# A 96-byte larger scratch tile ahead of the work area: every tile behind it moves by 96 bytes

## The reference

```
for layer in range(DEPTH):                      # DEPTH = 4
    g = norm_g[layer]
    ff = swiglu(rmsnorm(h, g[0]), ffn_w_in[layer, 0], ffn_w_out[layer, 0])
    h = h + 0.5 * rmsnorm(ff, g[1])
    u = rmsnorm(h, g[2])
    m = mixer(u)          # layers 0, 3: window attention; 1: gated linear attention; 2: rwkv
    h = h + rmsnorm(m, g[3])
    ff = swiglu(rmsnorm(h, g[4]), ffn_w_in[layer, 1], ffn_w_out[layer, 1])
    h = h + 0.5 * rmsnorm(ff, g[5])

def swiglu(x, w_in, w_out):                     # w_in 1024 x 5632, w_out 2816 x 1024
    gate, up = jnp.split(x @ w_in, 2, axis=-1)
    return (jax.nn.silu(gate) * up) @ w_out
```

## Time and profile before

| | |
|---|---|
| time, median of 3 | 3388.44 us (3382.83 to 3391.96) |
| the profiled execution's own time | 3391.96 us |
| its span | 3390.2 us |
| TensorE busy | 3270.2 us, 96% |
| VectorE, ScalarE, GpSimd busy | 1961.5, 1518.3, 175.0 us |
| chain that ended last | TensorE 85%, VectorE 8%, ScalarE 5% |
| transfers | 522.06 MB, mean 154 GB/s |

### The profile page before, as it was taken

The page is one execution under the profiler, slowest core; times in us unless marked ns, Lnnn a source line. Parts: engine busy times, 40 slices in busy tenths (PEclk is TensorE's granted clock), DMA queues, the critical chain, the costliest instruction groups (busy, mean ns, idle before and its releaser), DMA issues.

```text
span 3390.2 us, 49870 instructions
## 1 busy us (share of the span) xinstructions
PE 3270.2 (96%) x21454; PEld 2885.9 (85%) x21454; DVE 1961.5 (58%) x2964; ACT 1518.3 (45%) x2539; POOL 175.0 (5%) x201
## 2 busy tenths in 40 slices
PE   7999999999999999999999999999999999999998
PEld 7987998987898987687989988987878888887897
DVE  4556556558556555574565565565456556825777
ACT  4455444455445443113444464454544344524554
POOL 0000000003000000230000000000011000100100
PEclk9998999999999999999999999999999999999999
DMA  7562656555656544314556554551013333531452
GB/s 252 187 198 88 220 191 226 190 170 166 206 190 225 187 151 157 125 45 155 187 181 224 187 165 166 190 168 28 26 63 112 123 123 129 179 93 63 136 187 100
DMA packets 413481, 522.06 MB, mean 154 GB/s; under 512 B 41639, under 2 KB 355740, under 8 KB 413132
## 3 DMA queue, kind: packets, MB, share of 16 engines
q1 hardware_dynamic: 407376, 515.92, 45.9%
q0 software_dynamic: 816, 2.10, 0.2%
q10 hardware_dynamic: 5068, 0.85, 0.1%
HBM read 516.21 MB, written 2.10 MB: 153 GB/s over the span
## 4 chain that ended last, share of the span: by engine, by line
PE 85%; DVE 8%; ACT 5%; issue 1%; POOL 0%; ACTq 0%; DMA 0%; DVEq 0%; POOLq 0%
PE ps L187 24%; PE ps L189 24%; PE ps L188 23%; PE ps L179 5%; PE ps L1332 2%; PE ps L197 2%; ACT a L1352 1%; DVE small L1389 1%; DVE a L1385 1%; ACT junk L723 1%; PE ps L869 1%; ACT a L1364 1%; PE ps L2044 1%; DVE fast_xt L776 1%; DVE tmp L706 1%
## 5 line engine op out<-in xcount | busy, mean ns | idle before, releaser
L187 PE MATMUL ps<-a 128*128 128x256 f32 (+1 forms) x4832 | 1513.3, 313 | 23.6 <-DVE fast_xt L776 8.4
L189 PE MATMUL ps<-a 128*128 128x256 f32 (+1 forms) x4664 | 1451.4, 311 | 0.0
L187 PEld LDWEIGHTS ps<-a 128*128 128x128 f32 x4832 | 909.6, 188 | 85.7 <-DVE a L1062 11.0
L188 PE MATMUL ps<-fast_xt,a 128*128 128x256 f32 x3400 | 953.8, 281 | 0.0
L189 PEld LDWEIGHTS ps<-a 128*128 128x128 f32 x4664 | 882.1, 189 | 52.4
L992 DVE TENSOR_TENSOR a<-ring,a 128x1024 fp32r<-128x1024 f32 x594 | 693.5, 1221 | 343.5 <-ACT a L986 343.5
L986 ACT ACTIVATE a<-ring 128x1024 fp32r<-128x1024 f32 x594 | 586.7, 1049 | 231.1 <-PE ps L189 231.1
L188 PEld LDWEIGHTS ps<-fast_xt,a 128*128 128x128 f32 x3400 | 640.2, 188 | 7.4
L188 PE MATMUL ps<-a 128*128 128x512 f32 (+1 forms) x1368 | 526.9, 385 | 0.0
L188 PEld LDWEIGHTS ps<-a 128*128 128x128 f32 x1368 | 257.3, 188 | 43.0
L1094 ACT ACTIVATE tmp<-ps 128x256 f32<-128x256 f32 x176 | 67.6, 384 | 478.9 <-PE ps L189 478.9
(11 more groups left out here) (380 smaller groups left out, 3938.9 us busy)
## 6 DMA issues: line engine op xcount, KB each, us to landing
ring<-in_ffn_w_in_dram SPq DMA_DIRECT2D x218, 1024.0 KB, 7.4
ring<-in_ffn_w_out_dram SPq DMA_DIRECT2D x121, 1024.0 KB, 5.0
ring<-in_ada_w_dram SPq DMA_DIRECT2D x48, 1024.0 KB, 5.3
ring<-in_swa_w_qkv_dram SPq DMA_DIRECT2D x12, 1024.0 KB, 7.7
ring<-in_gla_w_in_dram SPq DMA_DIRECT2D x12, 1024.0 KB, 7.4
ring<-in_rwkv_w_rkv_dram SPq DMA_DIRECT2D x12, 1024.0 KB, 5.1
ring<-in_na_w_qkv_dram SPq DMA_DIRECT2D x12, 1024.0 KB, 6.2
ring<-in_swa_w_o_dram SPq DMA_DIRECT2D x8, 1024.0 KB, 5.3
```

Source lines behind the costliest of these rows:

```text
L187: pe.x.matmul(out, lh, rh, start=start and i == 0, stop=False)
L188: pe.x.matmul(out, lh, rl, start=False, stop=False)
L189: ins = pe.x.matmul(out, ll, rh, start=False, stop=stop and i == n - 1)
```

## The change

`small` is declared with 640 columns in place of 616. The columns added are used by nothing.

```
-        K.smallbuf = sb("small", 616)
+        K.smallbuf = sb("small", 640)
         K.sc32 = sb("sc32", 256)
         mod = sb("mod", 192)
```

## The result

| | before | after |
|---|---|---|
| median | 3387.22 us (3382.83 to 3391.96, 4 runs) | 3413.84 us (3409.39 to 3414.19, 4 runs) |
| profiled execution, its span | 3391.96, 3390.2 us | 3409.92, 3408.1 us |
| ratio | | 1.0076, 95% interval 1.006 to 1.0092 |

The changed kernel is slower by 26.6 us by the medians (20 to 31 by the interval) and by 17.9 us between the two profiled executions. The one of before happened to be the slowest of its four runs, the one of after is not among the four of the table and was quicker than all but one of them, so the two figures are not in conflict. The forecast was +20.0 us.

A forecast was written before the change was run, and what follows sets the result against it. The prediction took TensorE's back-to-back matmul pitch to bound the kernel. Its terms, 23.4 + 0 - 3.4 = +20.0 us on a median of 3388.4, gave 3408.4 us, with a range of 3325 to 3418 us.

The forecast's parts named there:

- What bounds: Whole kernel: TensorE, busy 96% of the span at full clock, is the bound; only the pitch between matmuls can change.
- FFN in, from 117.7 to 120.0 ns: 256-column matmuls with `fast_xt` moving and arena weights: 3392 triples go from 353.1 to 360.0 ns, +23.4 us.
- 512 columns in the arena, 0: 1304 triples of 512 columns with all operands in the arena: pitch stays 226.6 ns, 0 us.
- 512 columns mixed, -3.4 us: Projections, 432 triples with operands in arena and fixed tiles: 229.2 to 226.6 ns a matmul, -3.4 us.
- The sum: Whole kernel: 23.4 + 0 - 3.4 = +20.0 us, giving 3408.4 us from the median.
- The latent attention, 0: Latent attention heads: some go from unequal to equal halves and as many the other way, 0 us.
- by halves of 256 bytes: float32r matmuls: pitch goes by whether operands begin in equal halves of 256 bytes; relative place, chance 0.44.
- Plain float32 matmuls, VectorE, ScalarE: Plain float32 matmuls and work on VectorE and ScalarE: no effect of the address to be seen, 0 us.
- absolute place: Moving operands at a rounder address are read quicker: 3341.6 us for 256 columns alone (chance 0.24), 3308.6 for all (0.10).
- That nothing happens: Whole kernel: row differences have other causes, or gains and losses cancel; 3388 us, chance 0.17.
- Fixed-tile pitch everywhere: 512 columns slow with moving operands at 128, where the arena goes, and 256 columns at 120.0 ns: +47.1 us, 3435.5, chance 0.05.
- the room below: All float32r matmuls at the skill page's issue gap, 109.2 and 215.8 ns: -129 us, not claimed to be reached.

The follow-up runs named there:

- everything at 32: Kernel before with 40 columns of padding ahead of the ring and `small` at 640, so every tile begins at 32 over 256 bytes: ratio 1.0073, 3412.92 us.
- arena at 160: Kernel before with `small` at 648: arena begins at 160 over a multiple of 256 bytes, fixed tiles at 128; one run, 3402.44 us.
- arena at 96: Kernel before with `small` at 632: arena begins at 96 over a multiple of 256 bytes, fixed tiles at 128; one run, 3394.32 us.
- arena at 0: Kernel before with `small` at 672: arena begins at 0 over a multiple of 256 bytes, fixed tiles at 128; ratio 1.0003.

## Why the prediction was right, point by point

- What bounds: right. No instruction and no wait changed, TensorE's busy time took 16.2 of the 17.9 us, and moving tiles by nothing but padding moved the time by up to 1%. The clock was read too kindly: the prediction had it at 10 tenths or close in all 40 slices, and the page prints 9 and once 8.
- FFN in, from 117.7 to 120.0 ns: right, and in the sum at most 2 us too large. By single starts it is 5.76 - 5.65 = 0.11 us a block; the 17 blocks leave it 0.10 to 0.11 beside FFN out, so 20 to 22 us over 198 blocks. They hold 16 x 198 = 3168 of the 3392 triples; the other 224 were not read and would add about 1.5 us at the same rate, 21.5 to 23.5 in all. The forecast was 23.4. The run with everything at 32 shows its cause, that the place is relative, and the run with `fast_xt` alone moved shows which tile takes part.
- 512 columns in the arena, 0: right for the second model's FFN (1105 matmuls in 250 us both times), wrong for the FFNs. There the 12 of FFN out became longer, by 0.01 to 0.02 us a block, 2 to 4 us over 198. The groups show it too: L187 with 512 columns went from 536.0 to 538.1 us busy, L188 from 508.8 to 510.9, L189 from 508.0 to 508.5. The prediction took these matmuls one by one and put nothing in the sum for what the FFN in ahead of them does to the first ones.
- 512 columns mixed, -3.4 us: right in the pitches where they were read, 229.2 to 226.7 and 231.8 to 227.3 ns. The sum over all of them was not read.
- The sum: the blocks give 0.120 x 198 = 23.8 us, and with the 1.5 and the -3.4 about 22. The measured differences are 17.9 us between the profiled executions, of which the one of before had some 10 us at 1.2 GHz ahead of the earlier trace rows, and 26.6 between the medians. That +20.0 lies between them is partly luck: the main term may be up to 2 us too large, one of 2 to 4 was missing, and the runs of one kernel (3382.83 to 3391.96 us before) spread as widely as the two measured differences lie apart. The range, 3325 to 3418 us, held both signs and would have held a quicker kernel too; slower had a chance of only 0.49.
- The latent attention, 0: wrong in its working, though too small to matter. Head 1 became slower as forecast, but head 2 should have become quicker and stayed at 230 ns. With it falls the reading "by halves of 256 bytes" that I took from the earlier trace rows. The arena at 160 shows the same. The forecast did not hang on it, since after the change the remainders of all tiles are equal, not only the halves.
- Plain float32 matmuls, VectorE, ScalarE: right; 48 plain matmuls of the rwkv layer in a row take 20.87 us in both traces, and VectorE's busy time differs by 0.8 us in 1961.
- The rivals: absolute place fell with everything at 32 (1.0073 where it wanted 1 or less). That nothing happens fell with the result (1.0076, interval from 1.006). The Trainium skill's page "Advanced Engine Details and Errata", section "SBUF Cachelines", names only lines of 16 bytes; by that rule the time would have stayed, and the runs here disagree with it as the only rule. Fixed-tile pitch everywhere fell with the 1105 matmuls. Of the room below that the prediction marked, 109.2 and 215.8 ns, no run showed anything: the shortest pitches were 117.1 ns (arena at 96) and 226.6.

I was right with the main term for a reason that was half right. The rows said "alike is slow in 256 columns" (true, and as it turned out for the moving operands), and "halves decide in 512" (not true, by head 2).

## What to carry to other kernels

Where TensorE runs back to back with float32r, the byte at which a tile begins is a parameter of the kernel. At 256 columns two tiles that took turns as the moving operand were slowest when they began at the same remainder over 256 bytes. At 512 columns it was not so: the mixed matmuls of the attention output were quicker with everything at the same remainder (226.7 and 227.3 ns against 229.2 and 231.8). No rule found here gives the other values, so a layout is to be tried and not derived. A change of any tile's size moves all the tiles behind it, so a difference of under 1% after such a change may be the layout and not the change; compare at equal remainders, or read the pitch in a few blocks. Rows of the same operation on differently placed tiles, where a trace holds them, gave the sign and the size here.

## What the runs showed that I had not expected

- The same 48 matmuls took 5.62, 5.65, 5.69, 5.71 or 5.76 us by the places of three tiles, though all of these begin on multiples of 32 bytes in every case. The distance works in both directions, but not alike: 96 bytes ahead gave 5.65, 96 behind 5.71.
- A matmul's pitch depends on the ones before it. With the arena at 0 the twelve of FFN out took 2.72 us, and 2.76 when `xh` alone had moved, though their own operands stood at the same bytes. In the changed kernel they took 2.74, and 2.73 with `fast_xt` or `xh` moved.
- What in the hardware does this is open. Moving all tiles together changed nothing (5.76 and 2.74 us with everything at 128 and with everything at 32), so it goes by how places stand to each other; no run tells what makes the difference.
